# A three-block transformer kernel on one core: the first stage cut short, norms made by the stage that writes x, the output projection by columns, v in three passes

## The chip, the cores and the metric

The kernel is one program on one core of a Trainium2 chip. The metric is the device time of one execution in microseconds (us). Engines are named as in the profile: PE (TensorE), DVE (VectorE), ACT (ScalarE), POOL (GpSimd), SP (SyncE, which issues the transfers).

## What is computed

512 tokens x of width 1024 and 256 context tokens pass three blocks. All numbers are float32.

```python
# block 1 (first_block): modulation from c and c_ctx, a token mixer, a mixture of experts
mx = split(silu(c) @ w_ada + b_ada, 6)                 # w_ada: 1024 x 6144; mc likewise, from c_ctx
hx = rms_norm(x, g_pre_mix) * (1 + mx[1]) + mx[0]      # hc likewise, from ctx and mc
x = x + mx[2] * rms_norm(token_mixer(hx, hc), g_post_mix)
hx = rms_norm(x, g_pre_ffn) * (1 + mx[4]) + mx[3]
x = x + mx[5] * rms_norm(moe_ffn(hx), g_post_ffn)
# blocks 2 and 3 (second_block): layer 0 even_mixer, layer 1 diff_mixer
x = x + mixer(rms_norm(x, norm[layer])) @ w_out        # qkv, rope on q and k, masked softmax
u = causal_conv3(rms_norm(x, ffn_norm[layer]) @ w_up)  # w_up: 1024 x 5632
x = x + (silu(u[:, :2816]) * u[:, 2816:]) @ w_down
return rms_norm(x, final_norm)                         # after layer 1
```

`rms_norm(x, g)` is `x * rsqrt(mean(x * x) + 1e-6) * g`. Its first factor is one number per token, so a product with a matrix can take `x * g` and be multiplied by that number afterwards.

## The kernel before, in words

x lies in the core's memory as `m.x`, features on the 128 partitions, in KT = 8 tiles of 512 tokens and 256 context tokens (ALLT = 768 columns). The program is a row of stages, one function each. A stage opens its buffers, writes one instruction list for each engine, and ends at a barrier of all engines; inside it engines meet at semaphores. There is no scheduler: each engine runs its list in the order of the code. `with eng.Fori(...)` is a loop of the hardware.

A product in "three passes" splits both sides into a rounded part (`Split.high`, type fp32r, written by ACT) and the rest (`Split.low`, by DVE) and adds high x high, high x low and low x high. Such a matmul leaves one record in the trace; a plain float32 matmul leaves two.

The stages that the change touches:
- `load_and_modulation` (L267): SP loads `vec`, two of the twelve 2 MB blocks of `w_ada`, `const`, `rowv` and x, and then a block whenever one is used. `product` (L303) takes a block with `silu_c` as weights (two columns), ACT copies the row out (L334), `turn` (L311) turns it into columns, DVE adds the bias (L345). `modulation_gain` and `rms_norm` (L361) follow: squares on ACT (L382), their mean over features as a matmul with the constant `inv_d` (L403), root (L385), reciprocal (L411), scaling (L417) and, where the result is a `Split`, high (L396) and low (L423). `project_in` (L495) then loads its weights and starts.
- `mlstm` (L659): 32 subs (4 heads x 4 token tiles x 2 directions). After the scans PE spreads them over partitions (L854), and in the loop over subs PE makes `qk` (L872), turns the scores (L883) and multiplies them with v in `pv` (L895); DVE makes logits and scores (L806, L795) and, three subs later, reads the product in `finish` (L780, L782); ACT makes the exponentials and copies. DVE's end part (L827 to L839) needs a root from ACT (L741).
- `attention` (L1556): eight steps of two heads. `project(j, s, part)` makes q, k (L1627, three passes) and v (L1632, plain float32, tokens on the partitions) in the one bank BP = 7. DVE's `rotate` (L1741 to L1748) reads q or k out of it, ACT's `copy_v` reads v. The weights of step j + 2 are split by ACT (`high_parts`, L1714) and DVE (`low_parts`, L1785) at the end of step j.
- `project_out` (L916): the outer loop runs over input tiles k, and all eight banks are finished together at the end. The first block goes on using it.
- `conv_ffn` (L1890): 44 jobs in two parts. 12, then 10 "up" jobs of 2 x 8 x 3 matmuls (L1974) in a bank pair that alternates, each part followed by 8 "down" jobs (L1984). In an up job ACT and DVE convolve from the bank (L2008, L2042, L2045), gate (L2011, L2049) and split the hidden tile (L2013, L2052). The weights of job n + 1 are split during job n (L1998, L2028).
- After each `project_out` and each `conv_ffn` of the last two blocks an `rms_norm` stage runs alone.

## Time and profile before

| | us |
| --- | --- |
| device time, median of 3 runs | 3072.64 (3067.43 to 3078.56) |
| the profiled execution | 3073.34 |
| its span, first to last instruction | 3071.5 |
| matmul records on PE, share of the span | 2608.5 (85%) |
| DVE busy | 1631.6 (53%) |
| ACT busy | 1145.1 (37%) |

The granted TensorE clock is 0.914 of full in the mean. The experts, from 709 to 1401 us of the span, are not touched. Times of the timeline count from the span's start. The busy time of a group of matmuls is the time that its records cover together.

### The profile page before, as it was taken

How to read it: one execution, taken by the hardware profiler on the slowest of the kernel's cores; microseconds unless marked ns; L12 is line 12 of the kernel's file. 1: busy time of each engine (PE TensorE's matmuls, PEld its weight loads, DVE VectorE, ACT ScalarE, POOL GpSimd, SP SyncE). 2: the span in 40 equal slices, each digit the busy share in tenths (PEclk: the TensorE clock that was granted, in tenths of full speed). 3: DMA queues.
4: the chain of work that ended last, by engine and by line, in shares of the span. 5: the costliest groups of instructions: out<-in, count | busy, mean ns of one | idle time of the engine just before them, and what ended most of it. 6: DMA issues, size and time to landing. Idle time of an engine off the chain costs nothing. (4 is left out here: it accounts for less than half of the span.)

```text
span 3071.5 us, 31597 instructions
## 1 busy us (share of the span) xinstructions
PE 2608.5 (85%) x10942; PEld 1837.6 (60%) x10942; DVE 1631.6 (53%) x2690; ACT 1145.1 (37%) x1790; POOL 140.0 (5%) x138
## 2 busy tenths in 40 slices
PE   7699796568999999993499986999958884699998
PEld 1244365345676767672376765888846662488886
DVE  0229286435777777775455435635435555455353
ACT  0200253205666666662233234523222222344232
POOL 0000000001121212120000000000000000000000
PEclk9899788778999999996699988999979986899999
DMA  7320001035999999996111012232211101022222
GB/s 295 144 99 1 4 1 56 14 127 208 363 357 348 363 354 353 359 353 241 62 62 41 21 55 94 91 103 96 69 66 58 41 20 52 31 96 92 101 93 70
DMA packets 75102, 418.67 MB, mean 136 GB/s; under 512 B 17072, under 2 KB 17200, under 8 KB 38896
## 3 DMA queue, kind: packets, MB, share of 16 engines
q1 hardware_dynamic: 55696, 383.67, 33.8%
q0 software_dynamic: 19296, 33.60, 3.0%
q8 instruction: 61, 1.00, 0.1%
q14 instruction: 49, 0.40, 0.0%
HBM read 415.10 MB, written 38.80 MB: 148 GB/s over the span
## 5 line engine op out<-in xcount | busy, mean ns | idle before, releaser
L1372 DVE TENSOR_TENSOR w_gu_low<-raw,w_gu_high 128x1024 fp32r<-128x1024 f32 x264 | 322.5, 1223 | 121.8 <-ACT w_gu_high L1321 109.7
L1321 ACT ACTIVATE w_gu_high<-raw 128x1024 fp32r<-128x1024 f32 x264 | 279.8, 1060 | 108.5 <-PE banks L1277 107.7
L1974 PE MATMUL banks<-h_high,w_high 128*128 128x512 f32 x704 | 276.1, 392 | 48.3 <-DVE w_low L2028 48.3
L1974 PE MATMUL banks<-h_low,w_high 128*128 128x512 f32 x704 | 275.6, 391 | 0.0
L1974 PE MATMUL banks<-h_high,w_low 128*128 128x512 f32 x704 | 275.5, 391 | 0.0
L1289 PE MATMUL banks<-raw,act_t 128*128 128x512 f32 x528 | 237.6, 593 | 0.9 <-ACT act_t L1344 0.9
L1277 PE MATMUL banks<-w_gu_high,x_t_high 128*128 128x512 f32 x528 | 214.1, 406 | 2.0 <-DVE x_t_low L1379 2.0
L1277 PE MATMUL banks<-w_gu_high,x_t_low 128*128 128x512 f32 x528 | 208.0, 394 | 0.0
L1277 PE MATMUL banks<-w_gu_low,x_t_high 128*128 128x512 f32 x528 | 207.6, 393 | 0.0
L2028 DVE TENSOR_TENSOR w_low<-raw,w_high 128x2048 fp32r<-128x2048 f32 (+2 forms) x76 | 152.9, 2012 | 89.9 <-ACT w_high L1998 89.9
L1998 ACT ACTIVATE w_high<-raw 128x2048 fp32r<-128x2048 f32 (+2 forms) x76 | 128.0, 1684 | 177.2 <-PE banks L1984 157.8
L1974 PEld LDWEIGHTS banks<-h_high,w_high 128*128 128x128 f32 x704 | 133.3, 189 | 77.8 <-issue 50.0
L1632 PE MATMUL banks<-w_qkv,h 128*128 128x128 f32 x1024 | 133.5, 297 | 26.1 <-DVE k L1748 25.9
L1289 PEld LDWEIGHTS banks<-raw,act_t 128*128 128x128 f32 x528 | 95.2, 190 | 95.8 <-issue 94.7
L1974 PEld LDWEIGHTS banks<-h_low,w_high 128*128 128x128 f32 x704 | 133.3, 189 | 27.8
L1974 PEld LDWEIGHTS banks<-h_high,w_low 128*128 128x128 f32 x704 | 133.2, 189 | 27.8
L1632 PEld LDWEIGHTS banks<-w_qkv,h 128*128 128x128 f32 x1024 | 130.5, 212 | 29.6 <-DVE k L1748 29.6
L2008 ACT ACTIVATE conv<-banks,vec 128x512 f32<-128x512 f32 x88 | 67.9, 771 | 200.7 <-PE banks L1974 200.7
L1984 PE MATMUL banks<-hidden_high,w_high 128*128 128x512 f32 x352 | 137.2, 390 | 0.0
L1984 PE MATMUL banks<-hidden_high,w_low 128*128 128x512 f32 x352 | 137.0, 389 | 0.0
L1984 PE MATMUL banks<-hidden_low,w_high 128*128 128x512 f32 x352 | 136.9, 389 | 0.0
L1450 POOL DMA_INDIRECT x_rows<-h_rows,token_i x68 | 69.8, 1027 | 1230.4 <-DVE token_i L1400 1221.9
(310 smaller groups left out, 4636.3 us busy)
## 6 DMA issues: line engine op xcount, KB each, us to landing
raw<-in_w_e SPq DMA_DIRECT2D x198, 1024.0 KB, 8.4
raw<-in_w_up SPq DMA_DIRECT2D x44, 1024.0 KB, 4.8
w_ada<-in_w_ada SPq DMA_DIRECT2D x12, 2048.0 KB, 8.1
expert_rows<-y_rows SPq DMA_DIRECT2D x16, 1024.0 KB, 11.3
w_qkv<-in_w_even SPq DMA_DIRECT2D x8, 1536.0 KB, 6.3
raw<-in_w_down SPq DMA_DIRECT2D x16, 768.0 KB, 4.3
w_qkv<-in_w_odd SPq DMA_DIRECT2D x8, 1536.0 KB, 6.6
raw<-in_w_down SPq DMA_DIRECT2D x16, 640.0 KB, 3.8
```

What stands on the lines that cost most here:

```text
L1277: mm = pe.matmul(ps[:, BG, :], xp[:, k, :], wp[:, j, :], start=(k == 0 and i == 0), stop=(k == KT - 1 and i == 2))
L1289: mm = pe.matmul(ps[:, BY + n, :], at[:, k * P:(k + 1) * P], ex.chunk(GU + k, s)[:, half], start=(k == 0), stop=(k == 1))
L1321: act.activation(w_gu[c].high[:].rearrange("p j n -> p (j n)"), ex.chunk(c, s), ACT.Copy).then_inc(gu_high, 1)
L1372: dve.tensor_tensor(w_gu[c].low[:].rearrange("p j n -> p (j n)"), ex.chunk(c, s), w_gu[c].high[:].rearrange("p j n -> p (j n)").bitcast(F3 ...
L1450: pool.indirect_dma_start(xg[s][:], None, scratch["h_rows"], bass.IndirectOffsetOnAxis(ap=token_i[s][:, 0:1], axis=0), bounds_check=SEQ - ...
L1632: mm = pe.matmul(ps[:, BP, i * P:(i + 1) * P], m.h[:, kk, i * P:(i + 1) * P], w[s][:, 2, kk, :], start=(kk == 0), stop=(kk == KT - 1))
L1974: mm = pe.matmul(ps[:, 2 * s + c, :], wp[:, at:at + P], hp[:, k, :], start=(k == 0 and i == 0), stop=(k == KT - 1 and i == 2))
L1984: mm = pe.matmul(ps[:, 4 + s, :], wp[:, k * P:(k + 1) * P], hp[:, k, :], start=(k == 0 and i == 0), stop=(k == b - a - 1 and i == 2))
L1998: act.activation(w[s].high[:, 0:cols], raw[s][:, 0:cols], ACT.Copy).then_inc(high_done, 1)
L2008: act.activation(y[s][:, c, :], ps[:, 2 * s + c, :], ACT.Identity, scale=tap(t, c, 2), bias=tap(t, c, 3)).then_inc(tap0, 1)
L2028: dve.tensor_tensor(w[s].low[:, 0:cols], raw[s][:, 0:cols], w[s].high[:, 0:cols].bitcast(F32), ALU.subtract).then_inc(low_done, 1)
```

## The change

`load_and_modulation`, `modulation_gain` and `rms_norm` at the start become one stage, `prologue`. It loads x in eight pieces and four blocks of `w_ada`, makes the norm first and then four products. The other two thirds of `w_ada` are 16 parts of 1 MB and 256 columns, multiplied inside `mlstm` by `later_part`: two at its start, two between the row matmuls, ten in `pv` of the subs in `IN_UNITS`, and two at the end.

In the last two blocks `m.hs` holds `x * g` split, without the norm's factor, and `m.rstd` that factor. A new `split_norm` makes both once, for layer 0. From then on the stage that writes x makes them: the class `Tail`, called in `mix_out` (which takes the place of `project_out` there, with one bank per output tile and the weights laid out by column tile) and in the second part of `conv_ffn`. The factor is applied where products are read: in attention it is multiplied into the `rope` tables and onto v, in `conv_ffn` DVE copies each bank times `m.rstd` into `up`. v is made in three passes with features on the partitions, scaled into `v_turned` and turned by four transposes. `finish_out` scales and stores the result.

```diff
+def prologue(m, d):
...
+                for k in range(KT):
+                    sp.dma_start(m.x[:, k, :], d["x"][:, k * ALLT:(k + 1) * ALLT]).then_inc(x_in[k], 16)
+                for n in range(N_FIRST):
+                    sp.dma_start(w[n][:].rearrange("p k n -> p (k n)"), d["w_ada"][n]).then_inc(w_in[n], 16)
...
+                for n in range(N_FIRST):
+                    product(n)
+                    if n >= 1:
+                        turn(n - 1)
+                turn(N_FIRST - 1)
...
+                dve.wait_ge(std_done, 2)
+                dve.reciprocal(std[:], std[:]).then_inc(rstd_done, 1)
+                dve.wait_ge(rstd_done, 1)
+                for k in range(KT):
+                    dve.tensor_tensor(sq[:, k, :], m.x[:, k, :], std[:], ALU.mult).then_inc(unit_done, 1)
+                dve.wait_ge(parts_done, N_FIRST)
...
+                dve.wait_ge(unit_done, KT)
+                for k in range(KT):
+                    dve.tensor_scalar(m.h[:, k, 0:SEQ], sq[:, k, 0:SEQ], m.gain[:, k, 0:1], mod[:, k, 0:1], ALU.mult, ALU.add)
...
+        EARLY, LATE = 4, 2
+        IN_UNITS = [4, 6, 10, 12, 16, 18, 22, 24, 28, 30]
...
+                for n in range(N_LATER):
+                    if n >= 2:
+                        sp.wait_ge(aw_used, n - 1)
+                    sp.dma_start(aw[n % 2][:].rearrange("p k n -> p (k n)"), d["w_ada_later"][n]).then_inc(aw_in[n % 2], 16)
...
+                    if n in IN_UNITS:
+                        j = EARLY + IN_UNITS.index(n)
+                        dve.tensor_copy(ada_row[:, j, :], ps[0:2, BM, M_AT:M_AT + HALF]).then_inc(rows_kept, 1)
...
+                def later_part(n, bank):
+                    pe.wait_ge(aw_in[n % 2], 16 * (n // 2) + 16)
+                    for k in range(KT):
+                        mm = pe.matmul(ps[0:2, bank, M_AT:M_AT + HALF], cs[:, k, :], aw[n % 2][:, k, :],
+                                       start=(k == 0), stop=(k == KT - 1))
+                    mm.then_inc(aw_used, 1)
...
                     k0, w = keys(i, r)
-                    pe.wait_ge(st_done, n + 1)
                     if n >= 2:
                         pe.wait_ge(h_done, n - 1)
+                    if n in IN_UNITS:
+                        later_part(EARLY + IN_UNITS.index(n), BM)
+                    pe.wait_ge(st_done, n + 1)
...
+                pe.wait_ge(h_done, len(subs))
+                for n in range(N_LATER - LATE, N_LATER):
+                    later_part(n, BM + n % 2)
+                pe.wait_ge(rows_kept, len(IN_UNITS))
+                pe.wait_ge(row_copied, EARLY + LATE)
+                for t in range(2 * N_LATER):
+                    mm = pe.transpose(ps[:, 5, 2 * t:2 * t + 2], ada_row[:, t // 2, (t % 2) * P:(t % 2 + 1) * P], ident[0:2, 0:2])
+                mm.then_inc(parts_done, 1)
...
+def split_norm(m, name, at):
...
+                for k in range(KT):
+                    act.activation(sq[:, k, :], m.x[:, k, 0:SEQ], ACT.Square).then_inc(sq_done, 1)
+                for k in range(KT):
+                    if k == KT // 2:
+                        act.wait_ge(ms_done, 1)
+                        act.activation(m.rstd[:], ps[:, 0, :], ACT.Sqrt, bias=CONST.of(m.const, "eps")).then_inc(std_done, 1)
+                    act.activation(m.hs.high[:, k, :], m.x[:, k, 0:SEQ], ACT.Copy, scale=VEC.of(m.vec, name, at + k, 1)).then_inc(high_done, 1)
...
+    def on_scalar(self, act, j):
+        act.wait_ge(self.added, self.before + j + 1)
+        if j >= 2:
+            act.wait_ge(self.summed, j - 1)
+        act.activation(self.sq[j % 2][:], self.x(j), ACT.Square).then_inc(self.sq_done, 1)
+        if self.split:
+            act.activation(self.m.hs.high[:, j, :], self.x(j), ACT.Copy, scale=self.gain(j)).then_inc(self.high_done, 1)
+
+    def on_tensor(self, pe, j):
+        pe.wait_ge(self.sq_done, j + 1)
+        pe.matmul(self.m.ps[:, self.bank, :], CONST.of(self.m.const, "inv_d"), self.sq[j % 2][:],
+                  start=(j == 0), stop=(j == KT - 1)).then_inc(self.summed, 1)
+
+    def on_vector(self, dve, j):
+        if self.split:
+            dve.wait_ge(self.high_done, j + 1)
+            dve.scalar_tensor_tensor(self.m.hs.low[:, j, :], self.x(j), self.gain(j), self.m.hs.high[:, j, :].bitcast(F32),
+                                     ALU.mult, ALU.subtract)
+
+    def root(self, act):
+        act.wait_ge(self.summed, KT)
+        act.activation(self.m.rstd[:], self.m.ps[:, self.bank, :], ACT.Sqrt, bias=CONST.of(self.m.const, "eps")).then_inc(self.std_done, 1)
+
+    def invert(self, dve):
+        dve.wait_ge(self.std_done, 1)
+        dve.reciprocal(self.m.rstd[:], self.m.rstd[:])
...
+def mix_out(m, w_dram, src, name, at):
...
+                for j in range(KT):
+                    s = j % 2
+                    if j >= NB:
+                        pe.wait_ge(tail.added, j - NB + 1)
+                    pe.wait_ge(w_low, j + 1)
+                    for k in range(KT):
+                        if j == 0:
+                            pe.wait_ge(h_low, k + 1)
+                        for i, (wp, hp) in enumerate(w[s].passes(h)):
+                            mm = pe.matmul(ps[:, j % NB, :], wp[:, k * P:(k + 1) * P], hp[:, k, :],
+                                           start=(k == 0 and i == 0), stop=(k == KT - 1 and i == 2))
+                    mm.then_inc(made, 1)
+                    if j >= 2:
+                        tail.on_tensor(pe, j - 2)
+                tail.on_tensor(pe, KT - 2)
+                tail.on_tensor(pe, KT - 1)
...
+                    for kk in range(KT):
+                        for i, (wp, hp) in enumerate(ws[part].passes(m.hs)):
+                            mm = pe.matmul(ps[:, BP, :], wp[:, kk, :], hp[:, kk, :], start=(kk == 0 and i == 0),
+                                           stop=(kk == KT - 1 and i == 2))
                     mm.then_inc((q_made, k_made, v_made)[part], 1)
+
+                def turn_v(j):
+                    pe.wait_ge(vt_ready, j + 1)
+                    for i in range(TT):
+                        mm = pe.transpose(ps[:, BP, i * P:(i + 1) * P], vt[:, i * P:(i + 1) * P], ident)
+                    mm.then_inc(vt_turned, 1)
...
                     if more:
                         project(j + 1, 1 - s, 2)
                     product(j, 2 * j + 1 if not diff else j, s, 1 if not diff else 0)
+                    if more:
+                        turn_v(j + 1)
...
+                def scale_v(j):
+                    dve.wait_ge(v_made, j + 1)
+                    if not isinstance(j, int) or j > 0:
+                        dve.wait_ge(vt_turned, j)
+                    dve.tensor_tensor(vt[:], ps[:, BP, :], m.rstd[:], ALU.mult).then_inc(vt_ready, 1)
...
                     normalise(j, 0)
                     if more:
                         rotate(j + 1, 1 - s, 0)
+                    if g is not None:
+                        low_parts(j + 2, s, 0)
                     mask(j, g, 1)
                     normalise(j, 1)
                     if more:
                         rotate(j + 1, 1 - s, 1)
+                    if g is not None:
+                        low_parts(j + 2, s, 1)
+                    if more:
+                        scale_v(j + 1)
+                    if g is not None:
+                        low_parts(j + 2, s, 2)
...
+                for a in range(2):
+                    ins = dve.tensor_tensor(rope[:, a, :], rope[:, a, :], m.rstd[:], ALU.mult)
+                ins.then_inc(rope_set, 1)
+                dve.wait_ge(rope_set, 1)
...
-                        pe.wait_ge(conv_done, 2 * (PARTS[part][0] + j) + 2)
+                        pe.wait_ge(up_read, 2 * (PARTS[part][0] + j) + 2)
...
-                        act.wait_ge(*((up_made, t + 1) if c == 0 else (used, n + 2)))
+                        act.wait_ge(up_read, 2 * t + (c + 5))
                         act.wait_ge(gate_free, t + 1)
-                        act.activation(y[s][:, c, :], ps[:, 2 * s + c, :], ACT.Identity, scale=tap(t, c, 2),
+                        act.activation(y[s][:, c, :], up[s][:, c, :], ACT.Identity, scale=tap(t, c, 2),
...
+                        if part == 1 and j >= 1:
+                            tail.on_vector(dve, j - 1)
...
+                        dve.wait_ge(*((up_made, t + 1) if c == 0 else (used, n + 2)))
+                        dve.tensor_tensor(up[s][:, c, :], ps[:, 2 * s + c, :], m.rstd[:], ALU.mult).then_inc(up_read, 1)
+                    for c in range(2):
                         dve.wait_ge(tap0, 2 * t + c + 1)
-                        src = ps[:, 2 * s + c, :]
+                        src = up[s][:, c, :]
...
+        s1, sb1, _ = m.open()
+        with s1:
+            m.hs, m.rstd = Split(sb1, "h", [P, KT, SEQ]), sb1("rstd", [P, SEQ])
+            split_norm(m, "even_norm", 0)
+            for layer in range(2):
                 s2, sb2, _ = m.open()
                 with s2:
-                    m.h, m.hs = sb2("h", [P, KT, SEQ]), Split(sb2, "h", [P, KT, SEQ])
-                    rms_norm(m, m.x, m.hs, [(0, SEQ)], norm_gain(("even_norm", "odd_norm")[layer], 0), whole=m.h)
+                    o = sb2("o", [P, KT, SEQ])
                     attention(m, d, ("w_even", "w_odd")[layer], o, layer == 1)
-                if layer == 1:
-                    head_norm(m, o)
-                project_out(m, d[("w_eo", "w_oo")[layer]], o)
-            s1, sb1, _ = m.open()
-            with s1:
-                m.hs = Split(sb1, "h", [P, KT, SEQ])
-                rms_norm(m, m.x, m.hs, [(0, SEQ)], norm_gain("ffn_norm", layer * KT))
-                conv_ffn(m, d, layer)
-        s1, sb1, _ = m.open()
-        with s1:
-            y = sb1("y", [P, KT, SEQ])
-            rms_norm(m, m.x, y, [(0, SEQ)], norm_gain("final_norm", 0), out=out)
+                    if layer == 1:
+                        head_norm(m, o)
+                    mix_out(m, d[("w_eo", "w_oo")[layer]], o, "ffn_norm", layer * KT)
+                conv_ffn(m, d, layer, ("odd_norm", "final_norm")[layer], 0)
+            finish_out(m, out)
```

In the loop of `mlstm` the later parts stand between a turn of scores and the product of the sub before. PE before (`w_ada` is not there; `scores` are turned, `v` is multiplied with `scores_t`):

```order
L883 MATMUL banks<-const,scores_9 128x128 x5
L895 MATMUL banks<-v,scores_t_9 128x128 x5
L883 MATMUL banks<-const,scores_9 128x128 x4
L895 MATMUL banks<-v,scores_t_9 128x128 x5
L872 MATMUL banks<-k,q 128x512 x2
```

PE now, the same place (subs 4 and 5):

```order
L947 MATMUL banks<-const,scores_7 128x128 x5
L961 MATMUL banks<-v,scores_t_7 128x128 x5
L947 MATMUL banks<-const,scores_7 128x128 x4
L896 MATMUL banks<-w_ada_7,silu_c 2x256 x8
L961 MATMUL banks<-v,scores_t_7 128x128 x5
L936 MATMUL banks<-k,q 128x512 x2
```

The eight matmuls of L896 are new; nothing else moved.

In an up job of `conv_ffn`, DVE before (`ISA` rows are waits):

```order
L2042 ISA
L2042 SCALAR_TENSOR_TENSOR conv_27<-banks,vec,conv_27 128x511
L2045 ISA
L2045 SCALAR_TENSOR_TENSOR conv_27<-banks,vec,conv_27 128x510
```

DVE now:

```order
L2347 TENSOR_TENSOR up_23<-banks,rstd 128x512 x2
L2349 ISA
L2351 ISA
L2351 SCALAR_TENSOR_TENSOR conv_23<-up_23,vec,conv_23 128x511
L2354 ISA
L2354 SCALAR_TENSOR_TENSOR conv_23<-up_23,vec,conv_23 128x510
L2349 REGISTER_ALU
```

Both halves of the product are read before the first tap of either.

In a step of attention, DVE before, from the rotated k on:

```order
L1748 TENSOR_TENSOR k_23<-straight,crossed 128x512
L1801 ISA
L1801 COPY o<-banks 128x512
```

DVE now:

```order
L2020 TENSOR_TENSOR k_21<-straight,crossed 128x512
L2063 TENSOR_TENSOR w_k_low<-w_qkv_21,w_k_high 128x1024
L2059 TENSOR_TENSOR v_turned<-banks,rstd 128x512
L2063 TENSOR_TENSOR w_v_low<-w_qkv_21,w_v_high 128x1024
L2087 COPY o<-banks 128x512
```

The low parts of the next weights now stand inside the step, behind each rotation and behind the new scaling of v; before, those of q and k stood after the copy of `o`.

## Rows read from the trace of the kernel before

**Rows 1.** The page, busy us, share of the span and records of each engine.

```profile
PE 2608.5 (85%) x10942; PEld 1837.6 (60%) x10942; DVE 1631.6 (53%) x2690; ACT 1145.1 (37%) x1790; POOL 140.0 (5%) x138
```

**Rows 2.** Windows: stretch, its us, busy us (records) per engine, clock, DMA share, GB/s.

```profile
5.00:10.00 5.00, 0.00 (x0) 0.00 (x0) 0.00 (x0) 0.00 (x0) 0.00 (x0) 1.00 1.02 436
...
363.00:385.00 22.00, 21.64 (x48) 14.05 (x48) 0.21 (x1) 6.90 (x16) 0.00 (x0) 0.50 0.00 1
385.00:495.00 110.00, 93.14 (x498) 64.76 (x497) 91.93 (x353) 54.37 (x148) 0.00 (x0) 0.89 0.00 1
...
1838.00:1868.00 30.00, 8.74 (x16) 3.60 (x16) 13.56 (x17) 11.46 (x19) 0.00 (x0) 0.69 0.13 48
1868.00:2235.00 367.00, 361.61 (x1584) 298.67 (x1584) 182.11 (x186) 133.07 (x136) 0.00 (x0) 0.99 0.26 91
```

**Rows 3.** Timeline of PE, 0 to 160: start, us, engine, line, operation, idle before.

```profile
19.22 15.89 PE L303 MATMUL banks<-w_ada,silu_c 128*2 128x512 f32 x32 [19.22 <-ACT silu_c L328]
...
59.19 7.03 PE L303 MATMUL banks<-w_ada,silu_c 128*2 128x512 f32 x16
...
116.39 13.48 PE L403 MATMUL banks<-sq,const 128*128 128x512 f32 x32 [2.56 <-ACT sq L382]
152.44 7.79 PE L567 MATMUL banks<-h,w_in 128*128 128x512 f32 x13 [22.57 <-DMA w_in<-in_w_in]
```

**Rows 4.** Timeline of the mLSTM, PE and DVE.

```profile
434.33 1.28 PE L895 MATMUL banks<-v,scores_t 128*128 128x128 f32 x10
437.38 0.35 DVE L780 TENSOR_SCALAR hout<-banks,row_cols 128x128 f32<-128x128 f32 x1
...
489.26 0.35 DVE L782 SCALAR_TENSOR_TENSOR hout<-banks,row_cols,hout 128x128 f32<-128x128 f32 x1
495.52 0.25 DVE L832 RECIPROCAL rs<-rs 128x16 f32<-128x16 f32 x1 [0.37 <-ACT rs L741]
```

**Rows 5.** Attention: timeline, and the page's group of v's matmuls.

```profile
1625.96 0.69 DVE L1748 TENSOR_TENSOR k<-straight,crossed 128x512 f32<-128x512 f32 x1
1626.71 7.41 PE L1632 MATMUL banks<-w_qkv,h 128*128 128x128 f32 x64
...
1638.70 0.50 PE L1627 MATMUL banks<-h_high,w_q_high 128*128 128x512 f32 x1
...
1644.06 0.39 PE L1627 MATMUL banks<-h_high,w_q_low 128*128 128x512 f32 x1
...
2393.59 7.41 PE L1632 MATMUL banks<-w_qkv,h 128*128 128x128 f32 x64 [2.48 <-DVE k L1748]
...
L1632 PE MATMUL banks<-w_qkv,h 128*128 128x128 f32 x1024 | 133.5, 297 | 26.1 <-DVE k L1748 25.9
```

**Rows 6.** Timeline of one up job's end in the first FFN, ACT and DVE.

```profile
1961.79 0.78 ACT L2008 ACTIVATE conv<-banks,vec 128x512 f32<-128x512 f32 x1 [4.10 <-PE banks L1974]
1965.87 1.28 ACT L1998 ACT_TABLE_LOAD   x1
1967.16 1.92 ACT L1998 ACTIVATE w_high<-raw 128x2048 fp32r<-128x2048 f32 x1
1969.11 2.29 DVE L2028 TENSOR_TENSOR w_low<-raw,w_high 128x2048 fp32r<-128x2048 f32 x1 [2.41 <-ACT w_high L1998]
```

**Rows 7.** Timeline: first matmul of an output projection, and what surrounds the norms.

```profile
1789.86 2.50 PE L964 MATMUL banks<-h_high,w_high 128*128 128x512 f32 x5 [6.24 <-ACT w_high L941]
...
1857.49 4.90 DVE L423 TENSOR_TENSOR h_low<-sq,h_high 128x512 fp32r<-128x512 f32 x8
...
2252.57 4.89 DVE L423 TENSOR_TENSOR h_low<-h,h_high 128x512 fp32r<-128x512 f32 x8
...
3049.27 0.69 DVE L2036 TENSOR_TENSOR x<-banks,x 128x512 f32<-128x512 f32 x1 [6.11 <-PE banks L1984]
3051.43 7.13 PE L403 MATMUL banks<-sq,const 128*128 128x512 f32 x16 [2.20 <-ACT sq L382]
3059.32 3.35 DVE L411 RECIPROCAL rstd<-std 128x512 f32<-128x512 f32 x1 [9.36 <-ACT std L385]
```

353 lines of the change are left out of this document (246 added, 107 removed).

## The prediction

> **What bounds the kernel now.** I read the page's busy shares first, then the stage windows, then the timeline inside each stage the change touches. The page gives TensorE 85% of the span [rows 1]. That is a mean over stages of very different kinds, so it only says that a stage without TensorE work is a target. The windows show which these are [rows 2]: in the norm after an output projection (1838 to 1868) TensorE is busy 8.74 of 30 us; the FFN (1868 to 2235) is TensorE from end to end, 361.61 of 367 us; the mLSTM loop (385 to 495) has VectorE at 91.93 of 110 us and TensorE at 93.14. So time comes off where a stage vanishes; work moved into the FFN or the mLSTM loop has to be priced there.
>
> **1. First stage.** Before, twelve products of 16 records ran ahead of everything: 7.03 us each at the full clock, 15.89 us for the first two because the engine started cold [rows 3]. Then came gain and norm (matmuls 116.39 to 129.87), and the first input projection started at 152.44, after 22.57 us of idle TensorE of which some 8 are its own weights' arrival [rows 3]. Now the norm comes first and only four products follow. vec, const and x are 4.7 MB; at the 436 GB/s of 5 to 10 us [rows 2] they are in by about 13 us, and squares and mean matmuls run behind the arriving pieces of x. The 32 mean records took 13.48 us with a cold start [rows 3], so from about 9 us they end near 22. The four products add 4 x 7.3 (the pitch between two with a turn) = 29, the weights arriving every 4.8 us, thus hidden. Last copy, turn, gains and the eight writes of h: about 6. h is ready at 57, the projection starts 8 later, at 65 instead of 152.4: **-87**. Bounds: -92 (mean matmuls hidden under the arrival) and -80 (weights late, each product 2 us longer).
>
> **2. The sixteen later parts in the mLSTM.** A part is 8 matmuls of 256 columns, half a product: 3.5 us. Two run before the scan results are there (slack to 363, cost 1), two between the row matmuls. Ten stand in front of a `pv`. There the slack is small: the product that starts at 434.33 is over at 435.6 and is read at 437.38, 1.8 later [rows 4]. I take 1.5 hidden of a part's 3.5, so VectorE comes 2 later, and its copy of the row adds the 0.35 of such a read: 10 x 2.35 = 23. The last two wait for the last output (489.6) and must pass ScalarE's copies before the root that VectorE awaits at 495.52 [rows 4]: two parts and a copy are 7.5, the root came after 5.5, so +2, and +1 for the table load behind them. On the other side, the row matmuls ran 22 us at the half clock (363 to 385, TensorE busy 21.64, clock 0.50 [rows 2]) and the loop began on it; the first products of the program, of the same form as the parts, lifted the clock within two products [rows 3]. I count -3 for the rows (with two parts in them) and -3 for the loop's start. Sum 1 + 23 + 3 - 6 = **+21**. Bounds: +8 (parts fill idle TensorE) and +50 (parts at the half clock, fully exposed).
> The Trainium skill, TensorE: Matmul & The Clock Gate, Part 4, says transposes do not count as work for the clock; by it the parts, real matmuls among many transposes, would raise the clock and the term would be nearer its low bound. The trace shows the stretch at 0.50 but not why.
>
> **3. Norm before the first attention.** Now ScalarE's 24 passes (8 squares, 8 rounded products, root) and VectorE's low parts overlap, with one reciprocal. It ends some 6 us earlier than the five serial passes: **-6** (0 to -9).
>
> **4. Attention.** v: 64 records of 128 columns took 7.41 us [rows 5]. By the page's column the three-pass form looks dearer, but its records overlap: the 24 matmuls of q start at 1638.70 and end at 1644.45, 5.75 us [rows 5]. So v in three passes saves 1.7, and the four transposes give back 0.4 and a wait of 0.1 to 0.5 (VectorE's scaling, 0.69, lies beside the product). In the second attention v waits for the rotated k, 2.48 us idle [rows 5], and the chain q, rotate, k, rotate, v is the step; the extra VectorE low part (1.2) falls between rotate and mask, where VectorE has over 1 us. So -1.2 a step, 7 steps, and -3 at its start: **-11**. In the first attention the rotated k is ready at 1626.65 and v starts at 1626.71 [rows 5], no slack; six steps get a low part between q's rotation and the second mask, which delays that softmax and k's rotation by about 1.4, so the gain of six steps is eaten: -1 and -3 at the start, **-4**. Bounds for both: -25 and +10.
>
> **5. Output projections with the norm's sum.** The first matmul of the old one came at 1789.86 [rows 7]; now it needs a column block and its low part, +1. The 192 passes stay 46. Six of the eight mean matmuls go between products: 16 records took 7.13 us [rows 7], so 0.89 each, +5.2. After the last product: add 0.69, a square of about that size, mean 0.89, a copy and a table load of 1.28 that outlast it by 1, root 0.76 (from 3058.56 to 3059.32), reciprocal 3.35 [rows 6, 7]: 7.7 with the hand-overs. The stage ends at 1789.9 + 1 + 46.1 + 5.2 + 7.7 = 1849.9; before, the norm ended at 1857.49 + 4.90 = 1862.4 [rows 7]. **-12.5, twice: -25** (-32 to -16).
>
> **6. End of each FFN.** By the same terms 5.2 + 7.7 after the last product. The first FFN's last product ended just before 2234, and its norm at 2252.57 + 4.89 = 2257.5 [rows 7]: 23.7 becomes 12.9, **-11**. At the end of the program only the sum and root move; the eight scaled writes and the store stay: **-0.5**.
>
> **7. Inside the FFN.** Each of 44 up jobs gets two VectorE reads of a bank at 0.69. VectorE has room by share, but its program now waits for the second half's product before it does the first half's taps, so after a product 1.7 us more lie on the chain read, taps, gate, rounding, next weights' high and low. In a pair with table loads that chain went from 1961.79 to 1971.40, 9.6 us [rows 6], against a product of 48 matmuls x 0.228 (361.61 us over 1584 records [rows 2]) = 10.9. With 1.7 it is 11.3, and the lag it leaves makes about 0.9 per pair: 10 such pairs, 9 us. At the turn to the down jobs (36 and 30 matmuls, 8.2 and 6.8 us) the same chain is late by 1 and 2: 6 us. **+15**; bounds 0 and +45.
> Against the change speaks the Trainium skill, ScalarE: Activation LUTs, "What ACT_TABLE_LOAD costs": a drain of 1.38 us beside the load; by it these pairs would lose about 14 us more. The trace disagrees: the load of 1965.87 takes 1.28 and the next activation starts 0.01 later [rows 6].
>
> **Sum.** -87 + 21 - 6 - 15 - 25 - 11.5 + 15 = -108.5. The profiled execution took 3073.3 (span 3071.5), 0.7 above the median of 3072.64; so 2964.8 against it, and 2964 against the median.
>
> **The rivals.**
> (a) The FFN chain binds in every up job. Without the FFN's +15 the sum is 2949; a chain 3.1 us over the product's 10.9 costs 44 x 3.1 = 136 and gives 3085, slower; it decides from 3.0 over (124 plus the 9 that can be told). Against it: the table loads stand in 10 pairs alone, and the chain without one is 11.3 - 1.28 = 10.0 [rows 6]. Chance 0.03. A milder form, 1 us over in each job, gives 2949 + 44 = 2993: 0.12.
> (b) The mLSTM absorbs the parts badly: cold clock and each part exposed, +50 instead of +21: 2993. For it: the half clock of rows 2. Chance 0.12.
> (c) Everything overlaps: parts in idle slots, no FFN loss, -25 in attention: -87 + 8 - 6 - 25 - 28 - 11.5 = -149.5, 2924. For it: TensorE's modelled ends hide idle time in the loop. Chance 0.12.
> (d) v in three passes is slower. The page gives 133.5 us for all of v [rows 5], 8.3 a step, and 24 records of 0.39 would be 9.4: +1.1 and 0.9 for turn and wait, over 16 steps, is +32 where I have -15: 3011. Against it the start times of rows 5. Chance 0.03.
> (e) The change gives no time: that is (a) with a chain 2.6 to 3.0 us over the product, 115 to 132 us lost: within 9 us of 3073. Chance 0.02.
>
> **How the numbers follow.** My case has 0.56. Its own spread, with the bounds of terms 2, 4, 5 and 7 partly cancelling, is 2940 to 2990. Eight in ten needs the milder (a), (b) and most of (c): 2928 to 3000. A measurement of this kernel tells 0.3%, 9 us, from no change. Faster 0.95 (all but the strong (a) and (e), which leave 0.05), same 0.02, slower 0.03.
>
> **What would show it.** First projection matmul at 62 to 70 us; the mLSTM stage 15 to 30 us longer, with waits of the output rows on TensorE near the ten parts; the old norms' windows of 25 to 30 us gone, about 8 us between last product and reciprocal in their place; FFN matmuls with gaps of about a microsecond only in the pairs with table loads; the v group at 24 starts 0.23 apart. I am wrong if the FFN's matmuls wait in most jobs for the weights' low part, or if the first stage ends after 75.

## The result, and the profile after

| | before | changed |
|---|---|---|
| median of the runs beside the profile, us | 3070.94 | 2977.24 |
| lowest and highest, us | 3067.43 to 3078.56 | 2971.90 to 2983.49 |
| span of the profiled execution, us | 3071.5 | 2978.2 |
| mean granted clock | 0.914 | 0.922 |

The ratio is 0.969, with a 95% interval of 0.966 to 0.972. The forecast was 2964 with a range of 2928 to 3000: the sign and the range held, and 15 of the 108.5 us that were forecast did not come. The page of the changed kernel, beside [rows 1]:

```profile
PE 2591.7 (87%) x10494; PEld 1803.9 (61%) x10494; DVE 1705.4 (57%) x2781; ACT 1166.1 (39%) x1797; POOL 140.6 (5%) x138
```

TensorE lost 17 us of work and the span 93: most of the gain is idle time of TensorE. VectorE has 74 us more to do. Where it went shows when each stage is measured from TensorE's first matmul in it to its first in the next. "Forecast" is the sum of the prediction's terms for that stretch.

| stretch | before | changed | difference | forecast |
|---|---|---|---|---|
| start to the first input projection | 152.4 | 64.9 | -87.5 | -87 |
| inside the input projection | 191.2 | 193.1 | +1.9 | 0 |
| its end to the mLSTM's output projection | 169.5 | 201.1 | +31.6 | +21 |
| from there to the first attention | 992.9 | 986.4 | -6.5 | -6 |
| first attention, first to last matmul | 277.5 | 276.6 | -0.9 | -4 |
| from there to the first FFN | 88.6 | 76.0 | -12.5 | -12.5 |
| first FFN to the second attention | 394.9 | 388.5 | -6.5 | -3.5 |
| second attention | 294.3 | 292.9 | -1.4 | -11 |
| from there to the second FFN | 125.9 | 110.6 | -15.3 | -12.5 |
| second FFN to the end of the span | 384.3 | 388.0 | +3.7 | +7 |

The mLSTM and the two attentions carry the miss: the first came 10.6 us dearer than forecast, and the attentions gave 2.3 where 15 was forecast. With the 1.9 inside the input projection that is 25 us. The other stretches came 10 us cheaper than forecast, and this hides a part of the miss in the total. The timeline of TensorE, 0 to 66 us, beside [rows 3]:

```profile
9.31 13.24 PE L309 MATMUL banks<-sq,const 128*128 128x512 f32 x32 [9.31 <-ACT sq L337]
22.48 13.89 PE L315 MATMUL banks<-w_ada,silu_c 128*2 128x512 f32 x32
36.31 0.41 PE L322 MATMUL banks<-const,v 2*128 2x2 f32 x4
36.64 7.03 PE L315 MATMUL banks<-w_ada,silu_c 128*2 128x512 f32 x16
...
64.90 2.08 PE L590 MATMUL banks<-h,w_in 128*128 128x512 f32 x2 [12.85 <-DMA w_in<-in_w_in]
```

The 32 mean matmuls begin at 9.3 as x arrives, four products follow with next to no wait, and the projection starts at 64.9 where I had 65.

The changed kernel's windows, with the columns of [rows 2]: the spreading of the scans, the mLSTM loop, the first FFN, the second attention.

```profile
278.90:297.70 18.80, 18.70 (x81) 10.33 (x80) 0.00 (x0) 7.62 (x19) 0.00 (x0) 1.00 0.48 171
298.20:431.20 133.00, 129.62 (x656) 77.81 (x656) 89.41 (x326) 51.58 (x145) 0.00 (x0) 0.92 0.21 74
1798.20:2169.60 371.40, 368.12 (x1595) 300.71 (x1596) 209.88 (x235) 142.66 (x148) 0.00 (x0) 0.99 0.26 88
...
2186.60:2479.60 293.00, 240.69 (x880) 173.30 (x880) 163.91 (x354) 80.02 (x193) 0.00 (x0) 0.86 0.10 38
```

The loop took 103.3 us before (385.6 to 488.9) and takes 133.0 now, with TensorE busy 129.62: the parts have made TensorE its bound. The second attention is the stage whose clock stands out, 0.86. TensorE's clock has two levels, 2.4 GHz (1.00 in the windows) and 1.2 GHz (0.50), which is called the half clock below.

### The profile page after: what moved, and what is told of

It is laid out like the page before. It is cut to its first block and busy times, and to the rows that moved or that the text cites. A ratio compares the mean times of both kernels' runs of the same rounds, so it can differ in the third digit from the quotient of the medians.

```text
span 2978.2 us, 30493 instructions
## 1 busy us (share of the span) xinstructions
PE 2591.7 (87%) x10494; PEld 1803.9 (61%) x10494; DVE 1705.4 (57%) x2781; ACT 1166.1 (39%) x1797; POOL 140.6 (5%) x138
## 5 line engine op out<-in xcount | busy, mean ns | idle before, releaser
L1446 DVE TENSOR_TENSOR w_gu_low<-raw,w_gu_high 128x1024 fp32r<-128x1024 f32 x264 | 322.8, 1223 | 121.9 <-ACT w_gu_high L1395 108.5
L2309 ACT ACTIVATE conv<-up,vec 128x512 f32<-128x512 f32 x88 | 70.5, 815 | 185.5 <-DVE up L2347 185.5
L1351 PEld LDWEIGHTS banks<-w_gu_high,x_t_low 128*128 128x128 f32 x528 | 99.7, 189 | 22.8
L590 PE MATMUL banks<-h,w_in 128*128 128x512 f32 (+3 forms) x256 | 102.2, 562 | 12.9 <-DMA w_in<-in_w_in 12.9
```

What stands on the lines that cost most here:

```text
L590: mm = pe.matmul(bank[0:cols, 0:t[1]], wt(name)[:, k, j * P:j * P + cols], m.h[:, k, t[0]:t[0] + t[1]], start=(k == 0), stop=(k == KT - 1))
L1351: mm = pe.matmul(ps[:, BG, :], xp[:, k, :], wp[:, j, :], start=(k == 0 and i == 0), stop=(k == KT - 1 and i == 2))
L1446: dve.tensor_tensor(w_gu[c].low[:].rearrange("p j n -> p (j n)"), ex.chunk(c, s), w_gu[c].high[:].rearrange("p j n -> p (j n)").bitcast(F3 ...
L2309: act.activation(y[s][:, c, :], up[s][:, c, :], ACT.Identity, scale=tap(t, c, 2), bias=tap(t, c, 3)).then_inc(tap0, 1)
```

## The experiments

The ratio of every kernel is to the kernel before on the same chip. Two changed kernels may have run on different chips, so a difference between them of a few us is read from stage times, not from the medians. Stage times are measured as in the table. "Filler" is a row of matmuls whose results nobody reads.

### Filler in the waits of the second attention

What is behind the 0.86? In the changed kernel the 24 matmuls of k start like this (TensorE's timeline):

```profile
2300.25 0.50 PE L1891 MATMUL banks<-h_high,w_k_high 128*128 128x512 f32 x1 [1.96 <-DVE q L2020]
2300.59 0.40 PE L1891 MATMUL banks<-h_low,w_k_high 128*128 128x512 f32 x1
2300.82 0.39 PE L1891 MATMUL banks<-h_high,w_k_low 128*128 128x512 f32 x1
...
2301.81 0.63 PE L1891 MATMUL banks<-h_high,w_k_high 128*128 128x512 f32 x1
2302.23 0.63 PE L1891 MATMUL banks<-h_low,w_k_high 128*128 128x512 f32 x1
...
2312.01 0.77 PE L1891 MATMUL banks<-h_high,w_v_high 128*128 128x512 f32 x1 [2.06 <-DVE k L2020]
2312.57 0.63 PE L1891 MATMUL banks<-h_low,w_v_high 128*128 128x512 f32 x1
```

Start times are 0.23 apart at 2.4 GHz and 0.43 apart at 1.2 GHz. The clock falls inside k's product, behind a wait of 1.96 us for the rotated q, and is down again when v starts, behind a wait of 2.06. So k took 7.3 us in place of 5.7 here. Before, waits of 1.96 and 2.48 us stood there and the clock fell as well: of the seven k products five took 7.3, and four of the seven v products 9.0 to 10.3 in place of 7.4.

```diff
+                def warm(j, count, first=False):
+                    if not first:
+                        pe.wait_ge(o_copied, j)
+                    for i in range(count):
+                        pe.matmul(ps[:, BO, :], m.hs.high[:, 0, 0:P], m.hs.high[:, i % KT, :], start=True, stop=True)
...
                     else:
+                        if diff:
+                            warm(j, 16 if first else 6 + 2 * (part - 1), first)
                         pe.wait_ge(q_ready if part == 1 else k_ready, j + 1)
...
```

> The changed kernel, with matmuls of no use added on TensorE in the second attention only: 6 while it waits for the rotated q, 8 while it waits for the rotated k, 16 at each of the two waits of the first step, 6 and 20 in the last step's waits; results go into a bank that is free then. Theory 1: the products of k and v took 7.1 to 8.6 us in most steps where 5.7 is the time at the full clock, because the clock falls to 1.2 GHz after these waits; with filler they all take 5.7, the stage goes from 292.9 to about 270 us and the kernel from 2977 to about 2957. Rival A: the clock falls by itself in this stage, filled or not: products keep their 7 to 8 us, time 2977. Rival B: the filler outlasts the waits and costs: 2980 or more.

Measured: 2947.98 us, ratio 0.960 (0.957 to 0.962), 29 below the changed kernel; the stage took 265.0. Its window, and k's first matmuls:

```profile
2182.70:2447.70 265.00, 250.20 (x1036) 180.29 (x1036) 163.50 (x353) 80.37 (x193) 0.00 (x0) 0.99 0.11 42
```

```profile
2286.71 0.62 PE L1886 MATMUL banks<-h_high 128*128 128x512 f32 x2
2287.71 0.50 PE L1899 MATMUL banks<-h_high,w_k_high 128*128 128x512 f32 x1 [0.38 <-DVE q L2032]
2288.05 0.40 PE L1899 MATMUL banks<-h_low,w_k_high 128*128 128x512 f32 x1
...
2298.31 0.50 PE L1899 MATMUL banks<-h_high,w_v_high 128*128 128x512 f32 x1
```

TensorE did more and the stage was 28 us shorter: all k and v products took 5.7. With the waits filled the clock holds, so rivals A and B fall. The Trainium skill, TensorE: Matmul & The Clock Gate, "HAM oscillation — how this bites in real kernels", describes a kernel whose waits for transfers send the clock down each time. The changed kernel's trace agrees in part: its waits are for VectorE and shorter than that kernel's, 1.96 to 2.10 us in the steps, and the clock fell behind most of them and not behind all.

### The same filler on the kernel before, and v in three passes alone

> The kernel before, with the same filler matmuls in the second attention as in the run with filler on the changed kernel. If the clock is what varies, all products of k take 5.7 and of v 7.4 us: 18 us of excess in steps and some 4 in the last step and at the start go, the stage from 294.3 to about 272 us, the kernel from 3072 to about 3050. Compared with the changed kernel with filler, whose stage was 265.0, the difference is then the worth of v in three passes without the clock: 7 or 8 us if a step gains 1.2 (six steps) and the first one gains, near 0 by the rival. Rival on the clock: before, the falls have another cause, and the stage stays above 285.

Measured: 3049.80 us, ratio 0.993 (0.991 to 0.994), the stage 270.5 us. A step took 31.96 us (from 2330.04 to 2362.00); in the changed kernel with filler 31.28 (from 2246.36 to 2277.64). With the clock held, the three passes are thus worth 0.7 a step, where I had 1.2, and 5.5 in the stage, where I had 11.

Where is the rest of the 1.7 that a product saves? From the start of v to the next q a step is 1.24 us shorter, as forecast. But v now starts 10.6 us behind the start of k, and before it was 10.06. The rotated k is what v waits for. By VectorE's timeline a weight's low part (1.23) now lies between q's rotation and the softmax, and the waits behind that rotation that could take it up were 0.22 and 0.53, together not over 1. That reason was read, not tried.

The second kernel is the one before with the changed attention and nothing else (the norm's factor is an array of ones):

> The kernel before, with the changed kernel's attention alone: v in three passes with its transposes, the weights' high and low parts spread over the step; the norm is as before, and the factor it applies is one. At the full clock a step of the second attention took 31.95 us before and, where the clock held, about 30.8 in the changed kernel; a step of the first 32.1 and 31.9. Theory 1 (v in three passes gains 1.2 a step in the second attention and almost nothing in the first, and the clock's falls take a part of it back): first attention 277.5 to about 276.5, second 294.3 to between 286 and 293, kernel 3072 to about 3064. Rival (v in three passes is worth nothing itself, my 1.7 of saved product is eaten by turn, copy and waits): both stages within 1 us of before at equal clock, kernel 3072.

Measured: 3072.03 us against 3072.88, ratio 0.9995 (0.9986 to 1.0005). The first attention took 277.2, the second 295.1. Its window, and the one of the kernel before:

```profile
2269.20:2564.40 295.20, 242.57 (x880) 174.39 (x880) 163.83 (x354) 80.11 (x193) 0.00 (x0) 0.86 0.10 38
```

```profile
2267.10:2561.40 294.30, 244.21 (x1168) 191.18 (x1168) 146.09 (x336) 71.10 (x185) 0.00 (x0) 0.89 0.10 38
```

The granted clock is 0.86 against 0.89. Now all eight v products take 7.2 to 7.4 us in place of 5.7 (in five the clock is down from the start, in three it falls 1.1 to 1.2 us in), and five of the k products 8.4 to 8.7. So the saved work comes back as half clock. The time is the rival's, the reason is not: at a held clock the edit does gain. In the first attention a step took 31.9 (from 1576.12 to 1608.07) against 32.1 before; there v's wait is 0.95 to 0.98 us and the clock holds.

### The parts in the mLSTM loop, moved

```diff
-        EARLY, LATE = 4, 2
-        IN_UNITS = [4, 6, 10, 12, 16, 18, 22, 24, 28, 30]
+        EARLY, LATE = 4, 12
+        IN_UNITS = []
...
                 for n in range(N_LATER - LATE, N_LATER):
+                    if n >= EARLY + 2:
+                        pe.wait_ge(row_copied, n - 1)
                     later_part(n, BM + n % 2)
-                pe.wait_ge(rows_kept, len(IN_UNITS))
```

> The changed kernel, with the ten parts of the loop taken out of it and done with the last two after the loop. Theory 1 (in the loop TensorE had become the bound, a part costs nearly its own 3.55 us there, 2.9 after what idle time it fills): the loop goes back from 133 to 104 us, the end grows by 10 x 3.6 = 36, the kernel to about 2984. Rival (a part in the loop costs more by the waits and copies that it brings than by its matmuls): the loop falls by over 36 us, the kernel is at 2977 or below. The term of my prediction (2.35 a part in the loop) would make it 2989.

Measured: 2992.38 us, ratio 0.974 (0.972 to 0.976), 15 above the changed kernel. The windows of the loop and of what follows it, and TensorE's timeline behind the loop:

```profile
295.20:397.90 102.70, 91.69 (x496) 63.43 (x496) 86.48 (x317) 52.94 (x145) 0.00 (x0) 0.92 0.01 2
397.90:469.60 71.70, 48.38 (x241) 21.04 (x240) 13.75 (x60) 10.09 (x21) 0.00 (x0) 0.90 0.46 165
```

```profile
398.74 7.07 PE L896 MATMUL banks<-w_ada,silu_c 128*2 128x256 f32 x32 [0.82 <-DVE hout L830]
407.34 7.12 PE L896 MATMUL banks<-w_ada,silu_c 128*2 128x256 f32 x32 [1.53 <-DMA w_ada<-in_w_ada_later]
416.78 7.07 PE L896 MATMUL banks<-w_ada,silu_c 128*2 128x256 f32 x32 [2.32 <-DMA w_ada<-in_w_ada_later]
```

The loop without parts takes 102.7, 30.3 less. A little of that is clock: the half clock at the loop's start lasted 20 us in the changed kernel and 17 here. Three other runs with the ten parts had 17 us of it too and took 132.0 to 132.1; the kernel before had 20 and took 103.3. At equal clock the ten cost 29.3 to 29.8, so 2.9 to 3.0 each. That is my theory's 2.9, not the prediction's 2.35. Behind the loop each costs 4.4 (71.7 less 27.9, over ten), as pairs wait for their transfers. The loop was the better place.

```diff
-        IN_UNITS = [4, 6, 10, 12, 16, 18, 22, 24, 28, 30]
+        IN_UNITS = [0, 2, 4, 6, 10, 12, 16, 18, 22, 24]
```

> The changed kernel, with the ten parts in the mLSTM loop moved forward: in front of the products 0, 2, 4, 6, 10, 12, 16, 18, 22, 24 in place of 4 to 30. The loop's first 20 us (298 to 318) ran at the half clock. Theory 1: a part is work of the kind that lifts the clock (the two early parts did so for the row matmuls), so two parts in the first 15 us end the half clock early: the loop goes from 133 to about 127 us and the kernel to about 2971. Rival: the half clock at the loop's start lasts as long with parts in it, and the first parts then run at half speed themselves, 7 us each: loop 136 to 140, kernel 2981 to 2984.

Measured: 2974.41 us, ratio 0.968 (0.966 to 0.970), which can't be told from the changed kernel. The loop took 131.4, neither theory's 127 nor the rival's 136, and the first part in it 5.6 us in place of 3.6. How long the half clock lasts at the loop's start differs between executions of the same instructions: 20 us in the changed kernel (to 318), 7 us in the run with filler (to 308), which is the same code up to there and whose loop took 127.1. It lasted 14 us here, within that spread. This experiment is inconclusive; the transposes and parts of the loop's start don't let one say what raises the clock. The Trainium skill, TensorE: Matmul & The Clock Gate, Part 4, says that transposes don't count as work for it; no run here shows it.

### The order in the FFN, and its reads left out

```diff
                         dve.tensor_tensor(up[s][:, c, :], ps[:, 2 * s + c, :], m.rstd[:], ALU.mult).then_inc(up_read, 1)
-                    for c in range(2):
                         dve.wait_ge(tap0, 2 * t + c + 1)
```

> The changed kernel, with one line's order changed in both FFN: VectorE does the first half's taps before it reads the second half's bank. Theory 1: the 4.2 us of gaps between products (0.3 to 0.8 in pairs with table loads, 0.4 and 1.2 at the turns to the down jobs) come from the 1.5 us of taps that were pushed behind the second half's product; they vanish, each FFN goes from 371.3 to about 367.2 us (first to last matmul), the kernel to about 2969. Rival: the gaps come from the two added reads of 0.69 us, wherever the taps stand: gaps 2 to 4 us, kernel 2973 to 2977.

Measured: 3040.96 us, ratio 0.990 (0.988 to 0.992): 64 slower than the changed kernel. Theory and rival are both wrong. VectorE's timeline of one job, first of this kernel, then of the changed one:

```profile
1885.29 2.29 DVE L2332 TENSOR_TENSOR w_low<-raw,w_high 128x2048 fp32r<-128x2048 f32 x1 [2.41 <-ACT w_high L2297]
1887.50 0.69 DVE L2347 TENSOR_TENSOR up<-banks,rstd 128x512 f32<-128x512 f32 x1
1889.34 0.75 DVE L2350 SCALAR_TENSOR_TENSOR conv<-up,vec,conv 128x511 f32<-128x511 f32 x1 [1.15 <-ACT conv L2309]
1890.24 0.75 DVE L2353 SCALAR_TENSOR_TENSOR conv<-up,vec,conv 128x510 f32<-128x510 f32 x1 [0.15 <-DVE conv L2350]
1890.91 0.68 DVE L2347 TENSOR_TENSOR up<-banks,rstd 128x512 f32<-128x512 f32 x1
1892.74 0.75 DVE L2350 SCALAR_TENSOR_TENSOR conv<-up,vec,conv 128x511 f32<-128x511 f32 x1 [1.15 <-ACT conv L2309]
```

```profile
1887.27 2.29 DVE L2332 TENSOR_TENSOR w_low<-raw,w_high 128x2048 fp32r<-128x2048 f32 x1 [0.98 <-ACT w_high L2297]
1889.47 1.51 DVE L2347 TENSOR_TENSOR up<-banks,rstd 128x512 f32<-128x512 f32 x2
1891.39 0.75 DVE L2351 SCALAR_TENSOR_TENSOR conv<-up,vec,conv 128x511 f32<-128x511 f32 x1 [0.40 <-ACT conv L2309]
...
1899.36 2.29 DVE L2332 TENSOR_TENSOR w_low<-raw,w_high 128x2048 fp32r<-128x2048 f32 x1 [2.41 <-ACT w_high L2297]
```

By the time VectorE has split the next weights, both halves of the product lie in their banks: the two reads follow one another with next to no wait, so in the changed kernel nothing waits for the second half. ScalarE's first tap of each half (0.82) needs that half's read. Read together, the second half's tap runs beside the first half's taps on VectorE; read one by one, each costs VectorE 1.15 of waiting. That puts the chain above the product's 10.9 us in most up jobs: TensorE waited at 17 places in the first FFN and 19 in the second, 1.0 to 2.9 us at most of them, 25 and 28 us in all, where the changed kernel has six places and 3.3 us. Behind the longer waits the clock fell too: 16 us of half clock in an FFN in place of 5, which costs about 5 us more. Each FFN grew by 30.5 and 32.5 us (374.1 to 404.6 and 406.6, with its last mean matmuls). That is the milder form of the prediction's rival (a), about 1.4 us a job and not 3.1, set off by one line.

> The changed kernel, whose FFNs read the banks directly as before: the norm's factor is left out of the up products, and so are the two reads of 0.69 us in each of 44 jobs. Theory 1 (the chain of VectorE and ScalarE, lengthened by the reads, ends last only beside table loads): the gaps of 4.2 us vanish and each FFN goes from 371.3 to about 367 us (361.6 as before and 5.2 for the mean matmuls): span 2978 to about 2970. Rival (the mean matmuls and the down jobs in single steps cost more than 5.2, and the reads nothing): 369 to 371 us.

Measured: one execution, 2967.31 us, span 2965.5. The first FFN's window:

```profile
1795.10:2161.50 366.40, 366.37 (x1596) 301.00 (x1597) 183.69 (x191) 137.62 (x148) 0.00 (x0) 0.99 0.26 89
```

TensorE has no gap left. The window ends 0.6 us behind the last product: from the first to the last it is 365.8 us, and 366.3 in the second FFN, where the changed kernel has 371.3 in both. So the two added reads cost 5.5 and 5.0 us, and about 0.5 of the 5.5 is a shorter half clock at that FFN's start. What is left above the 361.6 of before [rows 2], 4.2 and 4.7, fits the five mean matmuls that lie between products, at 0.9 each. The reads' cost lies in the gaps that TensorE's timeline of the changed kernel puts down to the weights' low part:

```profile
1856.39 0.49 PE L2269 MATMUL banks<-h_high,w_high 128*128 128x512 f32 x1 [0.63 <-DVE w_low L2332]
1879.09 0.49 PE L2269 MATMUL banks<-h_high,w_high 128*128 128x512 f32 x1 [0.63 <-DVE w_low L2332]
...
2117.14 0.50 PE L2279 MATMUL banks<-hidden_high,w_high 128*128 128x512 f32 x1 [0.99 <-DVE w_low L2332]
```

Four of the five pairs with table loads have such a gap (0.15 to 0.65), and so has each turn from up to down jobs, behind the first down job (0.23 and 0.99).

### The norm's work behind the output projection

In `mix_out`, `tail.on_scalar`, `on_vector` and `on_tensor` are called for all eight columns after the last sum, and ScalarE waits for that sum:

```diff
-                for j in range(KT):
-                    if j >= 1:
-                        tail.on_scalar(act, j - 1)
-                    if j + 2 < KT:
-                        high(j + 2)
-                tail.on_scalar(act, KT - 1)
+                for j in range(KT - 2):
+                    high(j + 2)
+                for j in range(KT):
+                    act.wait_ge(tail.added, KT)
+                    tail.on_scalar(act, j)
```

> The changed kernel, where the two output projections of the last blocks do the norm's squares, rounded products, low parts and mean matmuls only after the last product's sum, and not beside the products. Measured for the changed kernel: 66.8 us from the first product of the second one to the first of its FFN (before, with stage by stage norms: 82.9), and 68.3 in the first (before: 82.3). Theory 1 (the gain comes from work that lies beside the products): 16 passes of ScalarE at 0.77 us, 12.3 us, less 1.2 of the last pair's that the changed kernel also has behind the last product, and the six mean matmuls no longer between products, -5.2: stage +6, kernel 2977 to about 2989. Rival (the gain is from columns in place of rows, one block in place of three, and the rstd left for the readers; what lies beside is worth little): stage within 2 us, kernel 2979.

Measured: 2983.04 us, ratio 0.970 (0.969 to 0.972), which the ratios alone can't tell from the changed kernel's 0.969 (0.966 to 0.972). The stages can: they took 71.4 and 70.2 us to their FFN, 3.1 and 3.4 more than the changed kernel's 68.3 and 66.8. ScalarE behind the last product:

```profile
2567.99 0.63 ACT L1690 ACTIVATE tail_sq<-x 128x512 f32<-128x512 f32 x1 [10.49 <-DVE x L1770]
2568.53 0.71 ACT L1692 ACTIVATE h_high<-x,vec 128x512 fp32r<-128x512 f32 x1
2569.14 0.61 ACT L1690 ACTIVATE tail_sq<-x 128x512 f32<-128x512 f32 x1
...
2577.77 0.69 ACT L1707 ACTIVATE rstd<-banks,const 128x512 f32<-128x512 f32 x1 [0.60 <-PE banks L1696]
```

The 16 passes take 1.13 a pair, 9.2 us in all and not 12.3, and 5.2 of mean matmuls leave the products. So of the 12.5 and 15 that each stage gained only about 3, net, come from lying beside products. The rest must be what the stage no longer has: two serial passes over x with the reciprocal between them, and a block of its own. That is what remains, read and not tried piece by piece.

### Filler at the starts, and a version of the best parts

> The changed kernel with filler in the second attention (2948.0 as measured) and more of it: 28 matmuls at the start of both attentions and of both FFNs, 16 at the start of both output projections, 16 at both waits of the first attention's first step; and in the mLSTM ScalarE takes the root before it copies the two late rows of parts. Theory: each of these stages began with 12 to 17 products at 0.43 us in place of 0.228, about 2.7 to 3 us; k and v of the first step lose 1.5 and 2.5. Two attentions 2.9 each, k and v 4, two projections 2.8 each, two FFNs 3 each: 21 us; and 4 for the root (first matmul of the mLSTM's output transposes 4 us earlier behind the loop): 2948 to about 2923. Rival: a filler that starts cold only moves the half clock into itself where it fits, and where the wait is shorter than the filler it delays the stage: gain under 8, 2940 or more.

Measured: 2935.89 us, ratio 0.956 (0.954 to 0.958), with the next one the fastest of the study: 41 below the changed one, 12 below the one with filler in the second attention alone, where I had 25. The root worked nearly as expected: the mLSTM's output transposes wait 3.7 us in place of 7.0, where I had 4 less.

```profile
428.29 7.07 PE L896 MATMUL banks<-w_ada,silu_c 128*2 128x256 f32 x32 [1.13 <-DVE hout L830]
435.92 2.10 PE L979 MATMUL banks<-const,ada_rows 2*128 2x2 f32 x32 [0.56 <-ACT ada_rows L744]
441.76 3.65 PE L986 MATMUL banks<-const,hout 128*128 128x128 f32 x16 [3.74 <-DVE hout L887]
...
1427.77 8.67 PE L1888 MATMUL banks<-h_high 128*128 128x512 f32 x28 [8.29 <-PEq L262]
1448.59 0.50 PE L1901 MATMUL banks<-h_high,w_k_high 128*128 128x512 f32 x1 [2.68 <-DVE q L2035]
```

The filler at stage starts gave about half its estimate; k of the first step still took 7.3 behind a wait of 2.68 that the filler left open. What each start gave by itself was not tried.

> The kernel with all the filler and the earlier root (2935.9 as measured), with three edits: the filler in the wait for the rotated k is 6 matmuls in place of 8 (8 ended 0.46 us after k was ready, in 7 steps: -3), and full-precision filler at the start of the input projection (12 matmuls) and of the mLSTM's output projection (7), whose first 4.5 and 7 us ran at the half clock: -2 and -2.5. Theory: about 2928, a ratio to before of 0.953. Rival (filler does not fit the first waits, whose length is that of a load): 2933 or more.

Measured: 2936.10 us, ratio 0.955 (0.953 to 0.956), no better. The full-precision filler at the input projection shows why:

```profile
57.79 13.05 PE L566 MATMUL banks<-x 128*128 128x512 f32 x24 [5.46 <-PEq L262]
70.67 9.61 PE L592 MATMUL banks<-h,w_in 128*128 128x512 f32 x22
```

Twelve such matmuls leave 24 records and took 13.05 us from a cold start; the stage began at 70.7 in place of some 65 and lost more than the clock gave. The filler at the mLSTM's output projection gave nothing either: from the last transpose in front of it to the stage behind it were 57.4 us, and 56.2 without. Fewer filler matmuls before v changed nothing: v still started 10.6 behind k, so my reading of the 0.46 as filler that ran over was wrong, and v's start is set by the rotated k.

## Why the prediction was right or wrong

The time came out 15 us above the forecast and inside its range, but terms 2 and 4 failed by 23 us together. That the total is nearer than that is partly luck: the first stage, the norm, the projections and the FFNs were each a little too dear in the sum.

- **Term 1, first stage (-87; measured -87.5).** Right, in each of its steps: mean matmuls in the shadow of the arriving x, two products in 13.89 us, two at 7.03, the projection 12.85 behind the last turn. The 1.9 us inside the projection are not the change's: 1.7 of them lie in eight matmuls on the half clock (0.83 in place of 0.61 us), and in five of the other runs with the new first stage the same eight took 0.61.
- **Term 2, parts in the mLSTM (+21; measured +31.6).** The size was off and the step is "I take 1.5 hidden of a part's 3.5". A part costs 2.9 to 3.0 in the loop, some 30 for ten, not 23. I read the slack behind one product, 1.8 us, as if each part had it anew; but TensorE's idle time in the loop was 11.0 us in all (102.70 less 91.69, in the window without parts), and 3.4 of it are still there with the parts (133.00 less 129.62): 0.8 is hidden of a part, not 1.5. The -3 for the loop's start did not come: the half clock stood there again, to 318 us. The -3 of the rows did: with two parts among them they took 18.8 us at the full clock, against 22 at the half. The end cost 3.6 (27.9 against 24.3), my +3; the run with the earlier root, 24.6, shows that it was ScalarE's order.
- **Term 3 (-6; measured -6.5).** Right in size; no run took it apart.
- **Term 4, attention (-15; measured -2.3).** The step that failed is the sum of full-clock durations in a stage whose clock stood at 0.89. The saved product is real, 1.7 us, but of the step's 1.2 only 0.7 stays with the clock held. For the rest "where VectorE has over 1 us" failed: VectorE had 0.75 to spare, and v starts 0.54 later behind k (a reading of the timelines). The falls of the clock took what was left: alone the edit moved nothing (0.9995). In the first attention I had "-3 at its start": the first step was 0.5 longer, as v's three passes began cold there too and then waited for their scaling and turn.
- **Term 5, output projections (-25; measured -27.8 with the head norm between).** Right in size. Its reason was right for the smaller part: work beside products is worth 3 of 12.5 to 15.
- **Terms 6 and 7, the FFNs (-11.5 and +15; measured -2.8 together, forecast +3.5).** The reads cost 5.0 to 5.5 in each, some 10 where I had 15; that leaves -13 for term 6. The place was right, gaps at the pairs with table loads and at the turns to the down jobs, their releaser the weights' low part. The reason, "its program now waits for the second half's product before it does the first half's taps", was wrong: the halves are both there, and the order I thought harmful is the one that keeps ScalarE's tap off the chain.
- **The rivals.** (a) did not occur, but one line's order brings its milder form: 3041 us. (b) overstated what happened: the mLSTM came 10.6 above the forecast, not 29. (c) fell with terms 2 and 4. (d) had v in three passes dearer by 32 us; it is a gain of 5.5 in the second attention at a held clock, and alone, with the falls of the clock, it is worth nothing either way. (e) fell.

## What to carry to other kernels

Price an edit in a stage with short waits of TensorE at the clock that stage has, not at the full one, and look at the start times inside a product behind each wait. Where VectorE or ScalarE sits between two products, a few matmuls of no use in the wait can be worth more than making the products cheaper: 28 us of 293 here, against nothing for v products that are 1.7 of 7.4 us shorter. When work is put into a loop that is bound by another engine, count that loop's idle time once for all of it. And where two halves each pass from one engine to another and back, do the first step of both halves before the next step of either: here the other order cost 64 us.

## What the runs showed of the hardware that was not expected

- Waits of 1.96 and 2.06 us between matmuls were enough to bring the granted clock from 2.4 to 1.2 GHz in most steps of the second attention. In the first, over the ten runs with three passes for v, waits of 0.94 to 1.28 did it in 6 of 60. The fall came in the wait or inside the product behind it, 1.5 us after its start in the row shown.
- The length of the half clock at the start of the mLSTM loop differed between executions of the same instructions, 20 and 7 us, and the loop with it by 6 (133.0 and 127.1).
- TensorE can be at work without a pause and stay at the half clock: before, in the row matmuls of the mLSTM, for 22 us (21.64 busy, clock 0.50 [rows 2]). All but the last of these us are matmuls of 64 rows by 256 columns and not transposes. In the changed kernel, with two parts in front of them and two among them, the same matmuls ran at 1.00 (18.8 us, the window above). Which of the two pairs did it was not tried.
- ScalarE's passes on 128x512 came 0.52 and 0.61 us after one another though their records are 0.61 to 0.71 long: 9.2 us for 16, where the records' sum is 10.6.
